# Recurrent layers: decays as running products by feature, built up from one token

## The reference, cut to what matters

```python
proj = h @ w_in; q, f, i, g = split(proj, 4)
q = silu(q); v = i
log_f = logaddexp(log(lb), log1p(-lb) + log_sigmoid(f))   # lb: lower bound by feature; 0 in layer 0
k = (1 - lb) * sigmoid(-f)
# o[t] = sum over s <= t of (q[t] * k[s] * exp(sum of log_f over s < u <= t)) @ v[s]
o = rmsnorm(o) ; return (o * silu(g)) @ w_out
```

## Time and profile before

| | us |
|---|---|
| median of 3 runs | 1173.41 (1173.29 to 1173.63) |
| span of the profiled execution | 1172.2 |
| the profiled execution's own time beside its span | only the span is listed; it is 1.2 us under the median of the runs |
| layer 0, first matmul of g0+1 to the first of the MLP | 23.88 to 170.04 |
| layer 3, the same from its first group's second part | 827.10 to 986.60 |

### The profile page before, as it was taken

How to read it: one execution, slowest core, us unless ns; L and a number is a source line. 1 busy time by engine, 2 the same in 40 slices (tenths; PEclk the granted TensorE clock), 3 DMA queues, 4 the chain that set the end, 5 groups by cost and what they waited for, 6 DMA issues and landing times.

```text
span 1172.2 us, 17197 instructions
## 1 busy us (share of the span) xinstructions
PE 1162.8 (99%) x6846; PEld 1030.6 (88%) x6846; DVE 795.5 (68%) x837; ACT 671.5 (57%) x797; POOL 23.1 (2%) x29
## 2 busy tenths in 40 slices
PE   9999999999999999999999999999999999999998
PEld 7999998888889989888888888888898999888886
DVE  6687777655656775756656875566888878665563
ACT  6965675444454545544546654455787566544443
POOL 1000000000001000000000000000000000000000
PEclk9999999999999999999999999999999999999999
DMA  9543335655466545654654646646543334654550
GB/s 342 185 144 108 109 108 190 234 186 176 182 218 170 177 140 166 211 197 163 211 198 146 219 175 215 215 144 214 179 124 129 108 109 144 198 200 177 184 192 36
DMA packets 86216, 202.92 MB, mean 173 GB/s; under 512 B 3357, under 2 KB 6503, under 8 KB 85904
## 3 DMA queue, kind: packets, MB, share of 16 engines
q1 hardware_dynamic: 86128, 202.10, 50.5%
q0 software_dynamic: 32, 0.03, 0.0%
HBM read 201.04 MB, written 1.08 MB: 172 GB/s over the span
## 4 chain that ended last, share of the span: by engine, by line
PE 93%; ACT 3%; DVE 2%; issue 1%; DMA 0%; POOL 0%; ACTq 0%; DVEq 0%
PE misc L619 10%; PE hb L619 10%; PE acc L671 10%; PE acc L672 10%; PE acc L673 10%; PE hb L624 5%; PE misc L624 5%; PE hb L565 4%; PE hb L566 4%; PE hb L563 4%; PE acc L843 2%; PE hb L580 2%; PE hb L578 2%; PE hb L579 2%; PE acc L831 1%; PE acc L832 1%
## 5 line engine op out<-in xcount | busy, mean ns | idle before, releaser
L1497 DVE TENSOR_TENSOR wlo<-raw,whi 128x2048 fp32r<-128x2048 f32 x184 | 416.7, 2292 | 139.8 <-ACT whi L1089 138.6
L1089 ACT ACTIVATE whi<-raw 128x2048 fp32r<-128x2048 f32 x183 | 342.6, 1905 | 121.3 <-PE acc L673 103.1
L671 PE MATMUL acc<-whi,arena_r 128*128 128x512 f32 x512 | 200.1, 391 | 0.0
L672 PE MATMUL acc<-wlo,arena_r 128*128 128x512 f32 x512 | 199.8, 390 | 0.0
L673 PE MATMUL acc<-whi,arena_r 128*128 128x512 f32 x512 | 199.5, 390 | 0.0
L619 PE MATMUL misc<-xhl,whi 128*128 128x512 f32 x512 | 122.7, 391 | 0.1
L619 PE MATMUL hb<-xhl,whi 128*128 128x512 f32 x512 | 122.7, 391 | 0.0
L673 PEld LDWEIGHTS acc<-whi,arena_r 128*128 128x128 f32 x512 | 96.2, 188 | 20.1
L671 PEld LDWEIGHTS acc<-whi,arena_r 128*128 128x128 f32 x512 | 96.2, 188 | 19.1
L619 PEld LDWEIGHTS misc<-xhl,whi 128*128 128x128 f32 x512 | 95.3, 188 | 20.0 <-DVE arena L1999 0.7
L672 PEld LDWEIGHTS acc<-wlo,arena_r 128*128 128x128 f32 x512 | 96.3, 188 | 18.8
(11 more groups left out here) (263 smaller groups left out, 1797.7 us busy)
## 6 DMA issues: line engine op xcount, KB each, us to landing
raw<-in_mlp_w_dram SPq DMA_DIRECT2D x128, 1024.0 KB, 5.4
raw<-in_a_w_in_dram SPq DMA_DIRECT2D x31, 1024.0 KB, 5.4
raw<-in_b_w_qkv_dram SPq DMA_DIRECT2D x12, 1024.0 KB, 7.2
raw<-in_a_w_out_dram SPq DMA_DIRECT2D x8, 1024.0 KB, 5.1
raw<-in_b_w_out_dram SPq DMA_DIRECT2D x4, 1024.0 KB, 5.0
arena<-in_x_dram SPq DMA_DIRECT2D x2, 512.0 KB, 5.3
raw<-in_a_w_in_dram SPq DMA_DIRECT2D x4, 256.0 KB, 5.3
arena<-in_decay_dram SPq DMA_DIRECT2D x1, 1024.0 KB, 12.1
```

The lines of the kernel that those rows point to most:

```text
L671: pe.matmul(o, ys, h, start=first and kt == 0, stop=False, skip_group_check=True)
L672: pe.matmul(o, ys, l, start=False, stop=False, skip_group_check=True)
L1089: act.activation(whi[:, g % 2, u, 0:n], raw[:, g % 2, u, 0:n], ACT.Copy).then_inc(hi_done, 1)
L1497: dve.tensor_tensor(wlo[:, g % 2, u, 0:n], raw[:, g % 2, u, 0:n], whi[:, g % 2, u, 0:n].bitcast(F32), ALU.subtract).then_inc(lo_done, 1)
```

## The change

The decay factors of a level are no longer sums of logarithms but running products. f itself (not its logarithm) is made with features on the partitions, next to k; for every block of m tokens its total, the product of f in it, is kept in a tree: `block_totals` on POOL makes the totals of level 2m from those of level m. Levels now go upward, 1, 2, 4, ..., 64, then the joining of the tiles. From level to level the key operand is multiplied in place by the total of the neighbouring block (POOL, `key_operands`), and the query operand likewise (DVE, `operands`). Since k is changed in place, ACT first copies a level's keys, in the order in which the product reads them, into a buffer (`k_pick`). The first query operand is q times f (`factors`, 1024 elements of each partition).

With that, `e_step`, `ex_step`, the decay table, its load and its rounding, `k_transposes` and `kT_copy` go. The order of the groups is f, q, f, q, v, v, g, g; the first four are of kind T, and the hand-written order covers 24 quarters, of g0+2 to g0+7. The lower bounds come in as 16 more rows of the gains and are worked on with 8 columns in place of 1024.

```diff
-        after_quarter = [(), (0, 1), (2, 3), (4,), (5,), (6, 7), (8,), (9,), (10, 11), (12,), (13,), (14, 15), (), (), (), ()]
+        after_quarter = {2: (0,), 3: (1,), 5: (2,), 6: (3,), 8: (4,), 9: (5,), 10: (6,), 11: (7, 8), 12: (9,), 13: (10,),
+                         14: (11,), 15: (12,), 16: (13,), 17: (14,), 18: (15,)}
...
-                    free = mixer_banks(layer, 4)
+                    free = mixer_banks(layer, 2)
...
-                        group("W", g0 + 1, 2, lambda k: None, need, first_norm, acc[2:4])
+                        group("T", g0 + 1, 2, free, need, first_norm)
                         pe.wait_ge(gains_sb, 2)
...
-                        group("W", g0, 0, acc_read, need, norm_steps(n), acc[0:2], early=True, half_used=unit_free)
-                        group("W", g0 + 1, 2, lambda k: None, need, banks=acc[2:4])
+                        group("T", g0, 0, acc_read, need, norm_steps(n), acc[0:2], early=True, half_used=unit_free)
+                        group("T", g0 + 1, 2, free, need)
...
                     def level_product(level):
                         if level >= 2:
                             wait_level_taken(pe, j, level - 2)
                         gb = acc[2 + level % 2]
-                        pe.wait_ge(p_done, 16 * j + level + 1)
-                        pq, pk = pair_ops[level % 2]
+                        pe.wait_ge(p_done[level // 8], 8 * j + level % 8 + 1)
+                        quad, lev = divmod(level, 8)
+                        if lev == 7:
+                            pe.wait_ge(k_done, 14 * j + 7 * quad + 7)
+                        else:
+                            pe.wait_ge(k_sb, 14 * j + 7 * quad + lev + 1)
...
+                                pk = pick[lev % 2][:, h * P:(h + 1) * P]
+                                pq = halves(flat_qf, at, LEVELS[lev], True, P)
...
                     def diagonal_products(quad):
-                        pe.wait_ge(kT_sb, 4 * (j + 1))
+                        pe.wait_ge(fk_done, 4 * j + 2 * (quad + 1))
                         pe.wait_ge(silu_done, 8 * j + 2 * (quad + 1))
...
+                    also = {2: lambda: diagonal_products(0), 11: lambda: diagonal_products(1), 17: lambda: quad_outputs(0),
+                            20: lambda: (quad_outputs(1), oms_step(0), oms_step(1)),
+                            22: lambda: (oms_step(2), oms_step(3))}
...
+                    for c, kind in enumerate("TTWWTT"):
+                        group(kind, g0 + 2 + c, 4 + 2 * c, free, need, some_steps, early=c == 2)
...
-            act.activation(decay[:, :, :], decay_in.rearrange("p (a b) -> p a b", b=P), ACT.Copy)\
-                .then_inc(decay_ready, 1)
...
+                    def f_a(b):
+                        if b < 2:
+                            act.wait_ge(f_z, 2 * j + b + 1)
+                        else:
+                            act.wait_ge(bank_free, free_count(layer) + b + 1)
+                        ln_1p_exp(scratch[b % 2][1], scratch[b % 2][0])
...
+                    f_a(0)
+                    split_unit(g0 + 2, 0, free=j + 1)
+                    f_a(1)
+                    f_b(0)
+                    split_unit(g0 + 2, 1)
+                    f_b(1)
+                    silu_a(0)
                     silu_b(0)
...
+                    for quarter in range(24):
+                        if quarter == 0:
+                            silu_a(1)
                         if quarter in (2, 4):
+                            f_a(1 + quarter // 2)
+                        if quarter in (6, 8):
+                            silu_a(quarter // 2 - 1)
+                        if quarter % 2 == 0 and quarter < 22:
+                            split_unit(g0 + 3 + quarter // 4, quarter // 2 % 2)
+                        if quarter == 0:
+                            silu_b(1)
+                        if quarter in (2, 4):
+                            f_b(1 + quarter // 2)
+                        if quarter in (6, 8):
+                            silu_b(quarter // 2 - 1)
+                        if quarter == 1:
+                            k_pick(0)
+                        if quarter == 10:
+                            k_pick(8)
+                        for level in after_quarter.get(quarter, ()):
+                            if level % 8 < 6:
+                                k_pick(level + 1)
...
+                    dve.wait_ge(rstd_ready, n + 1)
+                    f_a(0)
+                    f_a(1)
+                    split_unit(g0 + 2, 0)
+                    f_b(0)
+                    f_b(1)
+                    column(n)
+                    split_unit(g0 + 2, 1)
+                    if layer == 0:
+                        dve.wait_ge(gains_T, 2)
+                        ch.did(dve.tensor_copy(gains[:, 32:90], acc[2][:, 32:90]), gains_sb)
+                        ch.settle()
+                    f_c(0)
+                    f_c(1)
+                    silu_z(0)
+                    silu_a(0)
+                    silu_b(0)
+                    for quarter in range(24):
+                        if quarter == 0:
+                            silu_z(1)
+                        if quarter in (2, 4):
+                            f_a(1 + quarter // 2)
+                        if quarter in (6, 8):
+                            silu_z(quarter // 2 - 1)
+                        if quarter % 2 == 0 and quarter < 22:
+                            split_unit(g0 + 3 + quarter // 4, quarter // 2 % 2)
+                        if quarter == 0:
+                            silu_a(1)
+                            silu_b(1)
+                            factors(0)
+                        if quarter in (2, 4):
+                            f_b(1 + quarter // 2)
+                        if quarter in (3, 5):
+                            f_c(2 + quarter // 5)
+                        if quarter in (6, 8):
+                            silu_a(quarter // 2 - 1)
+                            silu_b(quarter // 2 - 1)
+                        if quarter == 9:
+                            factors(1)
+                        for level in after_quarter.get(quarter, ()):
                             if level == 8:
                                 part_tiles(0)
                             if level % 8 != 7:
+                                operands(level + 1)
                                 select(level)
...
+                        for m in LEVELS[:6]:
...
+                            ch.did(pool.tensor_tensor(to[:, there:there + count // 2], pairs[:, :, 0], pairs[:, :, 1],
+                                                      ALU.mult), tree_ready if m == 32 else None)
...
+                    block_totals(0)
+                    for lev in range(1, 5):
+                        key_operands(lev)
+                    block_totals(1)
+                    for lev in range(5, 8):
+                        key_operands(lev)
+                    for lev in range(1, 8):
+                        key_operands(8 + lev)
```

More of the change, by code:

```diff
@@ L35 @@
 MASKED = -1e30
[L36 removed]
+LEVELS = [1, 2, 4, 8, 16, 32, 64]
 WINDOWS = (2, 4, 8, 16)
@@ L43, in decay_sums @@
 def decay_sums():
[L48 to L57, removed]
+    return np.zeros((1, 1), np.float32)
 def level_masks():
@@ L181, in build_decoder @@
         ones = sb("ones", [P, P])
-        gains = sb("gains", [P, 74])
-        decay = sb("decay", [P, 16, P], F32R)
+        gains = sb("gains", [P, 90])
+        tree = sb("tree", [P, 2, 1008])
+        pick0 = sb("pick", [P, 512])
+        bounds = sb("bounds", [P, 5, HEADS])
         masks = sb("masks", [P, 10, P], U8)
@@ L1214, in silu_b, with silu_a @@
+                    def silu_a(b):
+                        act.wait_ge(bank_free, free_count(layer) + (1, 2, 5, 6)[b])
+                        ln_1p_exp(bank_of(qq, b).rearrange("p t h x -> p t (h x)"),
+                                  scratch[b % 2][0].rearrange("p (t x) -> p t x", t=TT))
+                    def silu_b(b):
                         after_dve()
-                        turn(act.activation(scratch[s][0], scratch[s][1], ACT.Exp))
+                        turn(act.activation(scratch[b % 2][0], scratch[b % 2][0], ACT.Exp))
@@ L1441, in _ @@
                     after_dve()
-                    turn(act.activation(lb_in, carve(10240, 2, D), ACT.Exp))
+                    turn(act.activation(bounds[:, 3:5, :], bounds[:, 1:3, :], ACT.Exp))
                 if g + 2 * NCH < n_groups:
@@ L1448, in _ @@
                     after_dve()
-                    turn(act.activation(lb_a, lb_a, ACT.Ln))
+                    turn(act.activation(bounds[:, 0, :], bounds[:, 0, :], ACT.Ln))
                 def y_copy(i):
@@ L1611, in _, with over_banks @@
                 if layer % 3 == 0:
[L1612 to L1622 removed]
+                    def over_banks(flat):
+                        return flat.rearrange("p (h t x) -> p h t x", h=2, t=TT)
@@ L1679, in gate_z @@
                             dve.wait_ge(diag_mm, 4 * j + 2)
```

(3 more changed lines are left out.)

564 lines of the change are left out of this document (201 added, 363 removed).

## The result

The changed kernel takes 1209.5 us (median of 4 runs, 1208.9 to 1209.9), the kernel before 1173.4 us beside it: 1.031 times as long, 95% interval 1.029 to 1.032. The profiled execution spans 1207.6 us. The forecast was 1208.5, and 1207.2 of span.

What follows compares the result with a forecast made beforehand. TensorE was taken to bound the kernel, busy 99% of the span. 1172.2 - 34.0 (its work) + 59.0 (waits) + 10.0 (GpSimd) = 1207.2 us of span, 1208.5 us median; range 1190 to 1234.

Steps and rivals of the forecast that it cites:

- TensorE's own work: Both mixer layers: 18.1 us a layer go, 1.1 are added, net 34 us less TensorE work.
- the strided operand: Level products' moving operand: taken as 0; at worst blocks of 1 and 2 double, 3 us a layer.
- the turn from W to T: Groups g0 and g0+1 change kind: 0.55 us more a group, 1.1 a layer.
- The new order of the lists: ScalarE's and VectorE's in-order lists make TensorE wait 29.3 us in layer 0, 29.6 in layer 3, 59 in all.
- The diagonals: TensorE's second wait, at diagonal_products(0) after quarter 2: there at 49.5, waits 4.8 us in layer 0.
- the walk: Timing the written engine lists entry by entry with instruction times from the profile; gave 59 us of waits, 10.0 more with GpSimd.
- GpSimd against VectorE: VectorE operations with two SBUF inputs wait until GpSimd's end: waits grow 4.3 us in layer 0, 5.7 in layer 3.
- The forecast's sign: In the mixers, each low half or operand beside a GpSimd operation takes longer than 2.29 or 0.7 us.
- Rival C: GpSimd's strided key operations take 2.0 us in place of 1.35: 15.7 us more, 1224 us; chance 22%.
- Rival D: Granted clock falls to 1.2 GHz after TensorE's long waits in the mixers: 8 us more, 1216 us; chance 18%.
- Rival A: List waits don't appear; TensorE loses 34 us of work, pays first waits alone (4.4 + 3.4): 1147 us; chance 6%.
- Rival B: GpSimd's operations hide fully in VectorE's idle time: 1198.5 us; chance 14%.

Runs made afterwards that it cites:

- lists_a: Changed kernel, same instructions, ScalarE's and VectorE's lists reordered in quarters 0 to 17, TensorE's level products a quarter later on average: 1149.0 us, ratio to before 0.979.
- lists_a_contiguous: lists_a with a contiguous moving operand in all level products (wrong elements, choice of blocks left out): 1147.9 us.
- split_first: Changed kernel with ScalarE's high half of the weights' rounding ahead of the sigmoid steps of quarters 0 to 8: 1174.5 us, ratio to before 1.0005.
- low_last: Changed kernel with VectorE's low halves of quarters 0 to 8 behind the sigmoid steps of their quarter: 1200.0 us.
- gains_first: Changed kernel with VectorE's copy of the gains and silu_z(0) ahead of the second low half of g0+2: 1205.3 us.
- few_keys: Changed kernel with GpSimd's key operations on 8 elements in place of 512, block totals kept: 1202.5 us.
- stay_busy: Changed kernel with TensorE filling its longest waits with matmuls that nobody reads: 1203.8 us.
- lists_a_few_keys: lists_a with GpSimd's key operations on 8 elements in place of 512: 1145.5 us.

## Why the prediction was right

The sum came out (1207.2 forecast, 1207.6 measured) and its mechanism is shown, but three of its terms were mis-sized in ways that cancel: that the total fits to 0.4 us is luck. The measured terms come from the starts of TensorE's instructions in the traces, counted from 0.4 us behind the first matmul of g0+1: a step over 0.55 us is counted as a wait of its length less 0.2, the rest as work. (Three steps of 0.57 to 0.59 us at the lower clock fall under it, 1.1 us in all, so the terms are good to about 1 us.) "Work" without half clock is read from lists_a, which has the same instructions. Layer 0's stage first, then from there to the end of layer 3's mixer.

| term | forecast | measured |
| --- | --- | --- |
| TensorE's own work | -34.0 | 145.7 to 131.2 and 815.5 to 802.1: -27.9 |
| waits, GpSimd's share in them | +59.0, +10.0 | 24.1 and 26.0, less 1.4 of before: +48.7 |
| the same work at the lower clock | 0 | 138.2 - 131.2 and 809.7 - 802.1: +14.6 |
| sum | +35.0 | +35.4 |

**TensorE's work.** The removed part was right: in layer 0 the decay sums take 16.5 us and the transposes 1.58 in the trace of before, 18.1 together. What was added was too small. The level products take 14.4 us in lists_a and 13.2 before; 0.9 of this is the strided operand, taken as 0 with the reason that such a product isn't bound by the fetch of a column. lists_a_contiguous shows that argument wrong for single elements (1.1 us in all, well under the 6 of the upper bound). The other 2.7 us of layer 0 are the turn from W to T, forecast at 1.1, and, it seems, that each product now stands alone between matmuls of weights, whose first step after it is 0.26 (T) or 0.32 us (W) on the mean, not 0.12 or 0.23. Before, this slower first step fell mostly on a decay sum (0.20 for 0.12) and went with it.

**The new order of the lists.** Right in place, releaser and size for most: start 4.4 forecast, 4.2 measured; level 1 5.9, 4.9; level 4 4.1 (5.3 with GpSimd), 4.3; level 5 6.5 (7.7), 5.3; level 10 0.5 (1.9), 1.2. The diagonals (4.8 and 1.7) and level 3 (2.6 and 0.8) waited less. TensorE, at the lower clock behind the wait before, came to the diagonals at 51.4 and not at 49.5, and the sigmoid was there at 53.2 and not at 54.2; for level 3 the same is likely, but wasn't taken apart. split_first, low_last and gains_first settle that the lists are the cause: three moves of single entries gave 35.0, 9.5 and 4.3 us where the walk said 34, 10.3 and 5.2.

**GpSimd against VectorE.** Forecast +10, few_keys says 7.0, which leaves out the block totals and what the short key operations still wait and block. (The four increases named for layer 0 add up to 4.1, not 4.3; it changes nothing.) The forecast's sign that each low half beside a GpSimd operation would be longer than 2.29 failed in the two mixers: there the low half had always begun first and took 2.28 or 2.29, and it was GpSimd that waited, 2.86 us at 117.40. The operands did lengthen, as forecast. Rival C's price was real for the blocks of 1 alone: 2.06 us at 55.32, with VectorE idle beside it, while the shortest were 1.15 us for blocks of 8 and 1.07 to 1.09 for larger ones; much of the mean of 1.64 is time held up by VectorE. VectorE's own operand for blocks of 1 took 1.14 (at 62.52), where the walk had 0.72. The Trainium skill's rule that reads with a wide step cost half again as much an element (GPSIMD Engine Reference, "Performance pitfalls for Q7 kernels") agrees with the trace for these blocks (2.06 against the contiguous 1.30, about 1.6 times), and no run shows it for others. All key operations together were worth 7.0 us by few_keys, not the 26 that this rival puts on GpSimd.

**The half clock.** Rival D's mechanism was real, though the forecast had set it at 0. Behind seven of the eight waits of over 3 us, and behind one of 2.9, the matmuls stepped at half rate for a while (from 40.28 to 45.5 behind the first), 14.6 us of slower steps in all. stay_busy takes them away and gains 5.7, near the 8 that the rival was priced at. The forecast hit in spite of that because its waits were too long by the part that the lower clock filled: waits and slow steps together are 63.3 against a forecast of 69.

**Rival A** asked for turns under 8 us and failed with 13.5, 10.9 and 11.0. Its 1147 is near what lists_a reaches (1149), by other terms: 27.9 us of work less and 3.4 of waits more, not 34 and 7.8. So the idle time of 34 and 44 us was room to be used, but only by another order. **Rival B** (GpSimd hides) is refuted by few_keys.

What stays open: GpSimd's 3.5 us in lists_a. 2.1 of them are the two waits that end with VectorE's operand for level 1 (0.8 and 1.3 us) and are gone in lists_a_few_keys; that operand took 1.68 us beside a key operation and 1.14 alone. How the rest divides into blocking and late keys was not separated, nor were the 2.7 us of TensorE's work taken apart.

## What to carry to other kernels

An engine with 30% of idle time can still be the one that makes the bound engine wait: walk the in-order lists entry by entry, and look first for a long operation that stands between two halves of a hand-over to another engine. Moving such operations ahead of the hand-over cost nothing and was worth 35 us here, the rest of the order 25 more; the work that a change removes from the bound engine shows only when the lists behind it are written for the new pace. And price waits as a chain, not as a sum: one taken away early mostly moves to the next.

## What the runs showed of the hardware

- After seven of eight waits of 3 to 7 us TensorE's matmuls stepped at half rate (0.21 for 0.12 us) for a while. The granted clock was 0.83 and 0.86 over the stretches with waits, 1.00 with the waits filled by idle matmuls.
- GpSimd and VectorE held each other up both ways when VectorE read two operands from SBUF: VectorE's operand of 0.69 us took 1.40 behind a GpSimd operation begun 0.23 us earlier, and GpSimd's total took 2.17 in place of 1.04 beside a low half begun earlier. VectorE's selection out of PSUM (L1657) took 0.73 to 0.75 us each of the 24 times, also beside GpSimd's operations.
- GpSimd's key operation on 512 elements took 1.07 to 1.09 us for large blocks, whose factor is repeated, less than its plain addition of 512 (1.30), and 2.06 for blocks of 1; with only 8 elements it took 0.20, and up to 2.03 beside a low half (0.57 on the mean). VectorE's query operand took 1.14 us for blocks of 1 and 0.69 for larger ones.
- A moving operand of single elements with a wide step makes eight 128-column matmuls take 1.19 us in place of 0.81, one of pairs 0.87, one of four or more 0.81.
